# A gated mixer's decays as running products, its small scores beside the projection, and eight conditioning products in the recurrent tail

## What is computed

```
q, f_fw, f_bw, i_in, g = split(h @ w_in, 5)
f = lb + (1 - lb) * sigmoid(f_logit);  k = 1 - f
b = cumsum(log f)                      # within chunks of 128 tokens
attn[t, s] = sum_d q[t,d] k[s,d] exp(b[t,d] - b[s,d])   for s <= t
o_fw = attn @ v + what the earlier chunk's state gives
o = rms_norm(o_fw + o_bw, norm_g) * silu(g);  x = x + g1 * (o @ w_out)
```

## Time and profile before

| | us |
|---|---|
| median of 3 runs | 2359.64 (2357.56 to 2362.45) |
| profiled execution: span | 2354.2 |
| profiled execution: its own time | not given by the page |
| TensorE busy | 2254.2 (96%) |
| VectorE busy | 1745.6 (74%) |
| ScalarE busy | 1300.1 (55%) |
| moved by DMA | 497.87 MB, 211 GB/s |

### The profile page before, as it was taken

How to read it: one execution, slowest core, us unless ns; L and a number is a source line. 1 busy time by engine, 2 the same in 40 slices (tenths; PEclk the granted TensorE clock), 3 DMA queues, 4 the chain that set the end, 5 groups by cost and what they waited for, 6 DMA issues and landing times. The chain is left out here.

```text
span 2354.2 us, 43875 instructions
## 1 busy us (share of the span) xinstructions
PE 2254.2 (96%) x14300; PEld 1892.0 (80%) x14300; DVE 1745.6 (74%) x3180; ACT 1300.1 (55%) x2124; POOL 430.1 (18%) x448
## 2 busy tenths in 40 slices
PE   7989989987999999999999999899999999999998
PEld 7657657863788889998888888588888999888886
DVE  6765775775578898886767668667888887667767
ACT  5543644565456675555454455746667555454544
POOL 0000000000012230003534330002223000335433
PEclk9999999999999999999999999999999999999999
DMA  8455555756357776557777785246777656877775
GB/s 247 172 215 164 182 200 200 282 220 229 127 175 236 234 228 200 188 184 243 242 240 242 242 264 190 107 161 189 234 235 227 191 186 191 257 241 243 241 240 171
DMA packets 248436, 497.87 MB, mean 211 GB/s; under 512 B 58616, under 2 KB 134648, under 8 KB 245008
## 3 DMA queue, kind: packets, MB, share of 16 engines
q1 hardware_dynamic: 248192, 496.29, 65.1%
q10 hardware_dynamic: 144, 0.26, 0.0%
HBM read 461.82 MB, written 34.65 MB: 211 GB/s over the span
## 5 line engine op out<-in xcount | busy, mean ns | idle before, releaser
L3004 PE MATMUL psum<-split_operands 128*128 128x512 f32 x3024 | 687.8, 389 | 0.0
L3004 PEld LDWEIGHTS psum<-split_operands 128*128 128x128 f32 x3024 | 567.4, 188 | 118.8 <-ACT split_operands L2946 0.8
L2983 DVE TENSOR_TENSOR split_operands<-weights_ring,split_operands 128x1024 fp32r<-128x1024 f32 x250 | 307.7, 1231 | 199.5 <-ACT split_operands L2946 199.5
L2946 ACT CAST split_operands<-weights_ring 128x1024 fp32r<-128x1024 f32 x252 | 265.3, 1053 | 328.1 <-PE psum L3004 326.9
L2741 DVE TENSOR_TENSOR split_operands<-weights_ring,split_operands 128x1024 fp32r<-128x1024 f32 x254 | 310.5, 1222 | 91.6 <-ACT split_operands L2658 90.8
L2930 POOL TENSOR_TENSOR arena<-arena,residual_gates 128x256 f32 (+1 forms) x254 | 275.0, 1083 | 406.3 <-DMA residual_gates<-expert_activations 400.7
L2588 PE MATMUL psum<-split_operands 128*128 128x512 f32 x1280 | 321.3, 393 | 2.8 <-ACT split_operands L2658 1.9
L2573 POOL TENSOR_TENSOR wide_sums<-wide_sums 128x256 f32<-128x256 f32 x160 | 133.3, 833 | 810.3 <-ACT wide_sums L2677 810.3
L2658 ACT CAST split_operands<-weights_ring 128x1024 fp32r<-128x1024 f32 x254 | 268.0, 1055 | 4.2 <-SPq L2559 2.1
L2588 PEld LDWEIGHTS psum<-split_operands 128*128 128x128 f32 x1280 | 230.1, 189 | 45.0 <-ACT split_operands L2658 2.3
L392 PEld LDWEIGHTS psum<-split_operands 128*128 128x128 f32 x1728 | 208.2, 192 | 6.2 <-DVE split_operands L408 2.4
(11 more groups left out here) (358 smaller groups left out, 2931.4 us busy)
## 6 DMA issues: line engine op xcount, KB each, us to landing
weights_ring<-in_peer_u_dram SPq DMA_DIRECT2D x256, 512.0 KB, 3.6
weights_ring<-in_peer_v_dram SPq DMA_DIRECT2D x256, 512.0 KB, 4.4
expert_activations<-residual_gates SPq DMA_DIRECT2D x256, 128.0 KB, 1.9
residual_gates<-expert_activations SPq DMA_DIRECT2D x256, 128.0 KB, 4.1
split_words<-in_w_ada_dram SPq DMA_DIRECT2D x20, 768.0 KB, 7.1
weights_ring<-in_w_in_dram SPq DMA_DIRECT2D x10, 1024.0 KB, 7.8
weights_ring<-in_hg_w_in_dram SPq DMA_DIRECT2D x10, 1024.0 KB, 6.4
arena<-in_hg_w_in_dram SPq DMA_DIRECT2D x10, 1024.0 KB, 5.2
```

Source lines behind the costliest of these rows:

```text
L2946: nc.scalar.copy(self.vs[:, s % 2, 0], self.v[:, s]).then_inc(self.v_high, 1)
L2983: nc.vector.tensor_tensor(self.vs[:, s % 2, 1], self.v[:, s], self.vs[:, s % 2, 0].bitcast(F32), ALU.subtract).then_inc(self.v_low, 1)
L3004: return K.nc.tensor.matmul(K.ps[:, 4 + 2 * t + half], gates[:, w, t * P:(t + 1) * P], v[:, wv, half * 512:(half + 1) * 512], start=(start ...
```

## The change

The decay from a token to the middle of its block is a product of f's. Instead of sums of logarithms and an exponential per level, the kernel keeps keys and queries as a state that already holds the decays for level L, and turns it into the state for 2L by multiplying one half of each block with the product of f over the neighbouring half (`update_keys`, `update_queries`, in place; 512 elements each per half of the heads and direction). The products of f over 2, 4, ..., 64 tokens come from pairwise multiplications (`span_products`). All runs for each half of the heads apart. f is now made on ScalarE in four pieces a block, keys as 1 - f too; ScalarE also copies the keys of both directions into one array a level (`MERGES`).

The projection's blocks are reordered (f, f, q for the first half of the heads, then for the second). The diagonal and the levels 1 to 16 are scored there: 12 sets of 32 matmuls (`SETS` at `SET_PLACES`), taken by VectorE at `TAKE_PLACES`. The attention stage keeps levels 32 and 64 and the crossing.

Of the 16 conditioning products of the attention stage 8 remain; four of their weight slices are loaded in the projection stage instead of two. The other 8 (blocks 8 to 11) are done in the recurrent tail ahead of gate unit 2 (`LateModulation`): two slices are loaded at the end of the recurrent projection, four at the tail's start and two into slots that come free; their rows are stored, read back as a column and a gate row, and the bias is added there and in the queries' projection. `ROW_PLACES` go from (4,5), (6,1), (7,3), (9,3) to (4,5), (6,7), (7,7), (9,1). Buffers of the arena are laid out anew.

```diff
-PRE = P + 1
-CROSS, DIAGONAL = 0, -1
-UNITS = [64, 32, 16, CROSS, 8, 4, 2, 1]
-SMALL = [DIAGONAL, 16, 8, 4, 2, 1]
-LOGARITHMS = [(4, 6), (4, 7), (5, 0), (5, 1)]
-SCANS = [(5, 2), (5, 6), (6, 4), (7, 0)]
-KEYS = [(5, 4), (6, 0), (6, 6), (7, 2)]
-DIAGONAL_KEYS = [(6, 1), (7, 3)]
-KEY_LOGARITHMS = [(6, 4), (6, 5), (7, 6), (7, 7)]
-FACTORS = [(7, 5), (7, 7), (8, 1), (8, 3)]
-FIRST_EXPONENTS = [(8, 5), (8, 7), (9, 1), (9, 3)]
-FACTOR_BUFFERS = 3
-ROW_PLACES = [(4, 5), (6, 1), (7, 3), (9, 3)]
+SMALL = [1, 2, 4, 8, 16]
+DIAGONAL = -1
+SETS = [(0, DIAGONAL), (0, 1), (0, 2), (0, 4), (0, 8), (0, 16), (1, DIAGONAL), (1, 1), (1, 2), (1, 4), (1, 8), (1, 16)]
+SET_PLACES = [(4, 0), (4, 0), (4, 5), (5, 2), (5, 7), (6, 7), (7, 2), (7, 2), (7, 7), (8, 4), (9, 1), (9, 6)]
+TAKE_PLACES = [(4, 4), (4, 4), (5, 1), (5, 6), (6, 4), (7, 1), (7, 6), (7, 6), (8, 3), (9, 0), (9, 5), (9, 7)]
+KEY_UPDATES = {(0, 1): [(4, 0), (4, 1)], (0, 2): [(4, 5), (4, 6)], (0, 4): [(5, 2), (5, 3)], (0, 8): [(5, 7), (6, 0)],
+               (1, 1): [(7, 0), (7, 1)], (1, 2): [(7, 7), (8, 0)], (0, 16): [(8, 3), (9, 0)],
+               (1, 4): [(8, 4), (8, 5)], (1, 8): [(9, 1), (9, 2)], (1, 16): [(9, 7), (9, 7)]}
+QUERY_UPDATES = {(0, 1): [(4, 2), (4, 3)], (0, 2): [(4, 7), (5, 0)], (0, 4): [(5, 4), (5, 5)], (0, 8): [(6, 2), (6, 3)],
+                 (1, 1): [(7, 4), (7, 5)], (1, 2): [(8, 1), (8, 2)], (1, 4): [(8, 6), (8, 7)],
+                 (1, 8): [(9, 3), (9, 4)], (0, 16): [(9, 5), (9, 6)], (1, 16): [(9, 7), (9, 7)]}
+MERGES = {(3, 2): (0, 1), (4, 4): (0, 2), (5, 1): (0, 4), (5, 6): (0, 8), (6, 6): (0, 16),
...
+          (6, 2): (1, 1), (7, 6): (1, 2), (8, 3): (1, 4), (9, 0): (1, 8), (9, 5): (1, 16)}
+SPAN_PLACES = [[(3, 1), (3, 2), (3, 2), (3, 3), (3, 3), (3, 3)], [(6, 1), (7, 2), (7, 2), (7, 3), (7, 3), (7, 3)]]
+START_PLACES = [[(3, 5), (3, 6), (3, 7)], [(6, 5), (6, 6), (6, 7)]]
+F_BLOCKS = [0, 1, 3, 4]
+Q_BLOCKS = [2, 5]
...
+def update_keys(K, H, half, L, d):
+
+
+    spans = H.f[:, half] if L == 1 else H.spans(half, L)
+    part = H.keys[:, half, d].rearrange("p (n s j) -> p n s j", s=2, j=L)[:, :, d]
+    other = spans[:, d].rearrange("p (n s) -> p n s", s=2)[:, :, 1 - d:2 - d].broadcast_to([P, HALF_STATE // (2 * L), L])
+    return K.nc.vector.tensor_tensor(part, part, other, ALU.mult)
...
+        for j, b in enumerate(F_BLOCKS):
+            half, d = j // 2, j % 2
+            if (n, k) in ((b + 1, 5), (b + 1, 6), (b + 1, 7), (b + 2, 0)):
+                i = (k - 5) % KD
+                if i == 0:
+                    act.wait_ge(self.product.proj_out, b + 1)
+                    if j == 0:
+                        act.wait_ge(self.bounds_ready, 1)
+                h = HG // 2 * half + i
+                f = H.f[:, half, d, i * CH * P:(i + 1) * CH * P]
+                ins = nc.scalar.activation(f, f, ACT.Identity, scale=self.lb[:, 1, h:h + 1], bias=self.lb[:, 0, h:h + 1])
+                if i == 3:
+                    ins.then_inc(self.f_ready, 1)
+            elif (n, k) == (b + 2, 1):
+                act.wait_ge(self.f_ready, j + 1)
+                nc.scalar.activation(H.keys[:, half, d], H.f[:, half, d], ACT.Copy, scale=-1.0, bias=1.0
+                                     ).then_inc(self.key_ready, 1)
+        if (n, k) in MERGES:
+            half, L = MERGES[n, k]
+            level = SMALL.index(L)
+            act.wait_ge(self.key_ready, 2 * half + 2)
+            act.wait_ge(self.keys_done[half], 2 * level)
+            act.wait_ge(self.scored[half], level + (level > 0))
+            out = H.merged[:, half].rearrange("p (b d j) -> p b d j", d=2, j=L)
+            nc.scalar.copy(out, crossed(self.K, H.keys_at + 2 * HALF_STATE * half, L, HALF_STATE)
+                           ).then_inc(self.merged[half], 1)
+
+    def pe(self, pe, n, k):
+        for g, (half, L) in enumerate(SETS):
+            if (n, k) == SET_PLACES[g]:
+                self.scores(pe, g, half, L)
+
+    def bank(self, g):
+        return self.K.ps[:, 6 + g % 2, 0:HG // 2 * CH * 32].rearrange("p (n t) -> p n t", t=32)
+
+    def scores(self, pe, g, half, L):
+        H = self.H
+        if L == DIAGONAL:
+            pe.wait_ge(self.diagonal_ready, half + 1)
+        else:
+            pe.wait_ge(self.merged[half], SMALL.index(L) + 1)
+            pe.wait_ge(self.queries_done[half], 2 + 2 * SMALL.index(L))
+        if g >= 2:
+            pe.wait_ge(self.small_out, g - 1)
+        for h in range(HG // 2):
+            for c in range(CH):
+                for b in range(4):
+                    cut = slice(32 * b, 32 * b + 32)
+                    at = (CH * h + c) * P + 32 * b
+                    if L == DIAGONAL:
+                        keys, queries = H.diagonal_keys[:, half, h, c, cut], H.q[:, HG // 2 * half + h, c, cut]
+                    else:
+                        keys = H.merged[:, half, at:at + 32]
+                        queries = crossed(self.K, H.queries_at + 2 * HALF_STATE * half + at, L, 32)
+                    last = self.K.nc.tensor.matmul(self.bank(g)[cut, CH * h + c], keys, queries, start=True,
+                                                   stop=True, tile_position=(0, 32 * b))
+        last.then_inc(self.scored[half], 1)
...
+    def take(self, dve, g, half, L):
+        nc, H, n = self.K.nc, self.H, HG // 2 * CH
+        small = H.small[:, n * half:n * (half + 1)]
+        dve.wait_ge(self.scored[half], 1 if L == DIAGONAL else 2 + SMALL.index(L))
+        if L == DIAGONAL:
+            nc.vector.tensor_copy(small, self.bank(g)).then_inc(self.small_out, 1)
+            return
+        dve.wait_ge(self.small_out, g)
+        mask = H.masks[:, SMALL.index(L)].unsqueeze(1).broadcast_to([P, n, 32])
+        nc.vector.copy_predicated(small, mask, self.bank(g)).then_inc(self.small_out, 1)
+
+    def span_products(self, link, half, level):
+
+
+        below = self.H.f[:, half] if level == 0 else self.H.spans(half, 1 << level)
+        below = below.rearrange("p d (n s) -> p d n s", s=2)
+        link(self.K.nc.vector.tensor_tensor(self.H.spans(half, 2 << level), below[:, :, :, 0], below[:, :, :, 1],
+                                            ALU.mult))
+
+    def first_state(self, dve, half, i):
+        nc, H = self.K.nc, self.H
+        if i == 0:
+            dve.wait_ge(self.product.proj_out, Q_BLOCKS[half] + 1)
+        if i < 2:
+            q = H.q[:, HG // 2 * half:HG // 2 * (half + 1)].rearrange("p h c t -> p (h c t)")
+            nc.vector.tensor_tensor(H.queries[:, half, 1 - i], q, H.f[:, half, i], ALU.mult
+                                    ).then_inc(self.queries_done[half], 1)
+            return
+        dve.wait_ge(self.key_ready, 2 * half + 2)
+        keys = H.diagonal_keys[:, half].rearrange("p h c t -> p (h c t)")
...
+        for g, (half, L) in enumerate(SETS):
+            if (n, k) == TAKE_PLACES[g]:
+                self.take(dve, g, half, L)
+        for (half, L), places in KEY_UPDATES.items():
+            for d, place in enumerate(places):
+                if (n, k) == place:
+                    level = SMALL.index(L)
+                    dve.wait_ge(self.merged[half], level + 1)
+                    if level == 0:
+                        dve.wait_ge(self.diagonal_ready, half + 1)
+                    dve.wait_ge(self.keys_done[half], 2 * level)
+                    update_keys(self.K, H, half, L, d).then_inc(self.keys_done[half], 1)
+        for (half, L), places in QUERY_UPDATES.items():
+            for d, place in enumerate(places):
+                if (n, k) == place:
+                    level = SMALL.index(L)
+                    dve.wait_ge(self.scored[half], 2 + level)
+                    dve.wait_ge(self.queries_done[half], 2 + 2 * level)
+                    update_queries(self.K, H, half, L, d).then_inc(self.queries_done[half], 1)
...
-            sp.wait_ge(product.w_low, KD * 9)
-            for m in range(2):
-                sp.dma_start(K.ring[:, 2048 * m:2048 * (m + 1)],
-                             K.i["w_ada_2"][1, m * P:(m + 1) * P, bass.ds(4 * 512, 2048)]
+            for m in range(4):
+                if m == 0:
+                    sp.wait_ge(row.w_used, KD)
+                elif m == 2:
+                    sp.wait_ge(product.w_low, KD * 9)
+                sp.dma_start(H.ada_ring[m], K.i["w_ada_2"][1, m * P:(m + 1) * P, bass.ds(4 * 512, 2048)]
                              ).then_inc(K.ada_loaded[m], 16)
             row.store(sp)
...
+            for half in range(2):
+                dve.wait_ge(scored[half], 1)
+                for d in range(2):
+                    update_keys(K, H, half, 32, d).then_inc(state[half], 1)
+                    update_queries(K, H, half, 32, d).then_inc(state[half], 1)
+            for half in range(2):
+                dve.wait_ge(scored[half], 2)
+                dve.wait_ge(state[half], 4)
+                crossing(half)
...
-            mod.load(sp, 2, 16)
+            mod.load(sp, 4, 8)
```

(57 more changed lines are left out.)

393 lines of the change are left out of this document (155 added, 238 removed).

## The result

The changed kernel takes 2327.82 us (median of 4 runs, 2325.78 to 2329.9), the kernel before on the same chip 2358.6 (4 runs): ratio 0.9875, 95% interval 0.9857 to 0.9892, 30.8 us faster. The prediction was 2332.5, 27.1 faster. The profiled execution has a span of 2326.7 us against 2354.2, and these 27.5 us can be placed, stretch by stretch. The page after, to be read beside the earlier trace rows: TensorE's busy time hardly changed, the span around it did.

The account below looks back on a forecast made before the run. TensorE, busy 96% of the span, bounds most of the kernel, but not the attention stage. Terms -44.1 + 9.8 - 0.7 + 3.0 + 1.0 + 1.0 + 2.9 = -27.1; 2354.2 - 27.1 + 5.4 = 2332.5 us, range 2321 to 2347.

Parts of the forecast that it names:

- Attention stage, -42.1 with clock and issue: Attention stage takes 15.3 us instead of 59.4 (-44.1), plus 1.0 for lower clock and 1.0 for issue gaps.
- Sets, +9.8 and -0.7: Projection: twelve sets cost 7.8 us and turns at ten places 2.0; two old stalls go, -0.7.
- Cover on VectorE and ScalarE: Projection: both engines keep up with TensorE, 1.5 us to spare at each of nine places; cost nothing.
- End of the projection, +3.0: Projection's end: stores wait behind conditioning loads on SP's queue; TensorE's gap to the next stage grows from 1.4 to 4.4 us.
- W + 2.5: Projection's end: SP may issue four conditioning loads 2.5 us after W, the end of step (9,1).
- Recurrent tail, +2.9: Recurrent tail: eight products enter ahead of unit 2, last two loads wait for buffers; unit 3's sigmoid comes 2.9 us later.
- A: Rival: VectorE becomes the projection's bound, 7.4 us late, and the attention chain adds 4.9; 2345 us, 13%.
- C: Rival: small matmuls don't overlap between the projection's, so the kernel is slower than before; 2372.6 us, 5%.
- B: Rival: the queue doesn't sustain 415 GB/s; projection ends 9.6 us later, attention stage 7.8; 2350 us, 8%.
- D: Rival: the stores at the projection's end overtake the loads; 2330 us, 6%.
- All high ends together: Whole kernel: every term at its upper bound (18; 13.6; 3.5; 3; 4.7; 5), given as 2351 us.

Follow-up runs that it names:

- e1: Changed kernel with the wait for the conditioning row's four stores moved from the projection's end to the attention stage's end; 2324.0 us.
- after_again: The changed kernel as it is, run again on another chip for comparison; 2328.0 us, ratio 0.9874 to the kernel before.
- e2: Changed kernel with eight instead of six buffers for the recurrent tail's conditioning loads; 2324.5 us, ratio 0.9867 to the kernel before.
- e3: Changed kernel with only the last matmul issued in ten of the twelve sets of small scores; 2321.5 us.
- e8: Changed kernel with each of the 48 updates preceded by a second identical product into scratch on VectorE; 2334.1 us.
- e1d: Changed kernel, stores on ScalarE's queue right behind the row's copies, ScalarE waiting for them before its last cast; one run, 2332.7 us.
- e5: Kernel before with only the move of eight conditioning products to the recurrent tail; 2359.7 us against 2354.8, ratio 1.0017.
- e4: Changed kernel with all 16 conditioning products in the attention stage, none in the recurrent tail; 2343.0 us, ratio 0.9941 to the kernel before.
- after: The changed kernel as first measured and profiled; 2327.82 us against 2358.6 for the kernel before, ratio 0.9875.
- e1c: Changed kernel with the four stores issued from ScalarE's queue right behind the row's copies, wait kept at the stage's end; 2324.4 us.
- e1b: Changed kernel with the four stores issued from ScalarE's queue behind its last output, wait kept at the stage's end; 2327.9 us.

## Why the prediction was right, and where a size was off

- **Attention stage, -42.1 with clock and issue: measured -42.7.** The order was as worked out, no load was waited for, and updates start 0.60 us apart. The terms inside were less exact than their sum. The lower clock takes up to 2.3 of the 16.7 us (scores 1.94 instead of 1.28 in e1, two products 3.57 instead of 1.9), where I had 1.0. Issue gaps take nothing in this profile, where I had 1.0; in after_again and e2 such a gap is there (0.67 and 1.18 us), and the stage is 17.6. That leaves 14.4 us or a little more for the work itself, where I had 15.3. That these three offset each other is luck.
- **Sets, +9.8 and -0.7: measured +8.7 in all.** 0.55 to 0.81 us each, 8.0 for twelve (forecast 7.8), and, by e3, 0.25 for a place whose set is nearly empty, against my 0.2 for the turn. The Trainium skill (TensorEngine Tiling (Array Packing), Key Properties) says that changing the tiling mode drains TensorE, and e3 shows the size of it: at most a quarter of a us both ways, between matmuls of 0.28.
- **Cover on VectorE and ScalarE: held**, and by more than I had thought: e8 adds 40 products of 0.60 us to VectorE in the projection for 1.6 us of time.
- **End of the projection, +3.0: measured +2.3.** TensorE ended 0.4 us later than worked out and the next stage began 0.3 us earlier (against the loads' first issue at 505.99, the prediction's W + 2.5). That the stores stand on the same queue was an incomplete reason: on an empty one (e1d) they still wait until 0.8 us before the loads are through. The price of the idle stretch is more than the gap: in the profiles e1's gap is 1.8 us shorter than after_again's and its attention stage another 1.2.
- **Recurrent tail, +2.9: the mis-sized term, +4.9 at the sigmoid and +4.4 in the span.** The loads came as predicted (two waits, the last load 22.5 us after the stage's start, predicted 22.2). Missing was the clock: after 2.1 us of waits among one-column products it dropped, which made the last product 0.85 and unit 2's first quarter 0.72 us longer. It doesn't always come: after_again waited as long and had no drop, and its +3.4 at the sigmoid (37.6) is near the forecast. e2 removes waits and drop.
- **The rest of the 3.7 us** between 27.1 predicted and 30.8 measured isn't a term: the profiled spans differ by 27.5, and unchanged stretches by 1.5 and 1.7 us with opposite signs. It is within the interval (0.9857 to 0.9892, 25 to 34 us).
- **Rivals.** A and C didn't come (e8, e3), nor B: 428 GB/s stood beside the end of the projection. D didn't: on the loads' queue the stores landed behind them, with a gap of 3.73.
- **A sum of mine was wrong.** All high ends together give 2347 us and not 2351 (2359.6 - 41.4 + 13.6 - 0.7 + 3.5 + 3 + 4.7 + 5, rounded). The range stated, 2321 to 2347, happens to end there.

## What to carry to other kernels

Take a stage apart by what ends its waits before moving work out of it: products that hide in waits cost time when moved alone (e5) and gain it once the waits are gone (e4 beside after). When a wait remains at a stage's end or a load comes late, look for the buffer or the wait that can be moved before accepting it: an edit of a few lines each gave about 4 us here, part of it TensorE's clock. And compare stretches rather than spans, as unchanged code moved by several us between executions.

## What the runs showed of the hardware

- Small stores wait long beside bulk loads even on a queue of their own, though they pass the last of the loads: 3.8 and 3.9 us from the first issue to the first packet (e1c, e1d), 5.1 us from the last issue to landing, while 424 GB/s flowed (mean of 511 to 518 us in e1d), against 0.9 us of waiting with no loads about.
- TensorE's idle time is paid twice: after 3.73 us of it the granted clock was 0.78 over 520 to 525 us and the first scores took 1.94 us; after 2.09 us of it (e1c) they took 1.62, after 1.64 us of it (e1) 1.28.
- The same code with nearly the same waits came out with and without a clock drop. The tail's second wait was 1.40 to 1.42 us in nine executions. Six had the drop (after, e1, e1b, e1c, e1d, e5; first wait 0.57 to 1.02, sigmoid at 39.1 to 39.4), three had none (after_again, e3, e8; first wait 0.50 to 0.72, sigmoid at 37.3 to 37.6). The lengths of the waits alone don't decide it, and what does wasn't tried.
- A burst of 128 records of small matmuls followed by products leaves an issue gap in some executions (after_again, e1, e2, e1c: 0.67, 0.96, 1.18, 0.29) and none in others (after, e3, e4). after and after_again are the same kernel, so it isn't the code alone. It wasn't tried what decides this.
